# Output projections of two token blocks as seven quarter products, with bias additions ahead of the query norms

## What is computed

```python
h = rms_norm(x, g1);  q | k | v | p = h @ w_in
a = windowed_attention(rms_norm(q), rms_norm(k), v, sinks)        # 2048 x 512
m = multiscale_pool(p, pool_w, pool_b, pool_scale)                # 2048 x 512
x = x + concat([a, m]) @ w_out                                    # w_out 1024 x 1024
x = x + conv_glu(rms_norm(x, g2), w_up, conv_w, conv_b, w_down)   # d_ff 2816
```

## Time and profile before

| what | value |
|---|---|
| median of 3 runs | 1769.95 us (1769.0 to 1771.88) |
| profiled execution | 1768.54 us |
| its span, first to last instruction | 1766.7 us |
| busy: PE, DVE, ACT, POOL | 1755.5, 1283.8, 810.7, 311.3 us |
| granted PE clock | 1.000 over the whole span |
| DMA | 328.02 MB, 186 GB/s on average |

### The profile page before, as it was taken

One profiled execution on the slowest core, in us unless ns is written; L12 is line 12 of the kernel. 1 busy time (PEld: TensorE's weight loads), 2 busy tenths in 40 slices (PEclk: granted clock), 3 DMA queues, 4 the chain that ended last, 5 costly groups with the idle time before them and its releaser, 6 DMA issues.

```text
span 1766.7 us, 23461 instructions
## 1 busy us (share of the span) xinstructions
PE 1755.5 (99%) x8502; PEld 1463.1 (83%) x8502; DVE 1283.8 (73%) x1725; ACT 810.7 (46%) x1440; POOL 311.3 (18%) x296
## 2 busy tenths in 40 slices
PE   9999999999999999999999999999999999999999
PEld 7788888888888888888888888888888888888887
DVE  4645634635789888889888878878878778765774
ACT  4554544534765444444554444444444433333321
POOL 2355224216110000000000000000004023210210
PEclk9999999999999999999999999999999999999999
DMA  8865382484446433332375232232237999976884
GB/s 325 279 230 187 110 322 105 175 305 141 166 168 241 152 96 120 131 96 72 132 267 186 84 94 74 78 94 79 72 97 241 339 363 313 309 252 220 295 286 131
DMA packets 214323, 328.02 MB, mean 186 GB/s; under 512 B 13945, under 2 KB 106305, under 8 KB 214209
## 3 DMA queue, kind: packets, MB, share of 16 engines
q1 hardware_dynamic: 194782, 274.04, 46.7%
q10 hardware_dynamic: 19427, 52.49, 7.5%
HBM read 254.13 MB, written 72.35 MB: 185 GB/s over the span
## 4 chain that ended last, share of the span: by engine, by line
PE 95%; ACT 2%; DVE 1%; POOL 1%; DMA 0%; issue 0%; SPq 0%; ACTq 0%; DVEq 0%
PE ps L879 31%; PE ps L881 30%; PE ps L880 30%; ACT xs L1363 1%; PE ps L1080 1%; PE ps L1130 1%; PE ps L1067 1%; PE ps L1056 1%; PE ps L951 0%; DVE w_lo L1652 0%; DMA raw<-in_w_in_dram 0%; POOL ss_q L2171 0%; PE ps L1043 0%; POOL rstd L2171 0%; DVE mx L1843 0%
## 5 line engine op out<-in xcount | busy, mean ns | idle before, releaser
L879 PE MATMUL ps<-va_hi,wv 128*128 128x512 f32 x1232 | 479.4, 389 | 0.0
L881 PE MATMUL ps<-va_hi,wv 128*128 128x512 f32 x1232 | 479.3, 389 | 0.0
L880 PE MATMUL ps<-va_lo,wv 128*128 128x512 f32 x1232 | 479.3, 389 | 0.0
L881 PEld LDWEIGHTS ps<-va_hi,wv 128*128 128x128 f32 x1232 | 231.3, 188 | 48.1
L879 PEld LDWEIGHTS ps<-va_hi,wv 128*128 128x128 f32 x1232 | 231.3, 188 | 48.0
L880 PEld LDWEIGHTS ps<-va_lo,wv 128*128 128x128 f32 x1232 | 231.3, 188 | 47.7
L879 PE MATMUL ps<-dt_hi,ds_hi 128*128 128x512 f32 x616 | 239.6, 389 | 0.0
L880 PE MATMUL ps<-dt_lo,ds_hi 128*128 128x512 f32 x616 | 239.6, 389 | 0.0
L881 PE MATMUL ps<-dt_hi,ds_lo 128*128 128x512 f32 x616 | 239.6, 389 | 0.0
L1975 DVE SCALAR_TENSOR_TENSOR cb<-ub,cst,cb 128x1024 f32<-128x1024 f32 x176 | 218.9, 1285 | 7.8 <-ACT cb L1489 7.8
L1489 ACT ACTIVATE cb<-ub,cst 128x1024 f32<-128x1024 f32 x88 | 109.3, 1244 | 157.6 <-DVE ub L2024 91.7
(11 more groups left out here) (186 smaller groups left out, 2821.3 us busy)
## 6 DMA issues: line engine op xcount, KB each, us to landing
dg<-gT_d SPq DMA_DIRECT2D x264, 256.0 KB, 5.2
rw<-in_w_up_dram SPq DMA_DIRECT2D x84, 512.0 KB, 5.1
dw<-in_w_down_dram SPq DMA_DIRECT2D x132, 256.0 KB, 5.5
gT_d<-cb ACTq DMA_DIRECT2D x44, 512.0 KB, 2.6
w_hi<-wA_d SPq DMA_DIRECT2D x30, 512.0 KB, 4.1
w_lo<-wA_d SPq DMA_DIRECT2D x30, 512.0 KB, 5.8
raw<-in_w_out_dram SPq DMA_DIRECT2D x20, 512.0 KB, 4.5
n<-in_x_dram SPq DMA_DIRECT2D x16, 512.0 KB, 7.5
```

The lines of the kernel that those rows point to most:

```text
L879: pe.matmul(out_ap, l_hi, r_hi, start=first, stop=False, skip_group_check=True)
L880: pe.matmul(out_ap, l_hi, r_lo, start=False, stop=False, skip_group_check=True)
L881: return pe.matmul(out_ap, l_lo, r_hi, start=False, stop=last, skip_group_check=True)
```

## The change

Blocks 1 and 2 no longer take the eight units of `o`. With the block's activations as two token halves by two channel halves, and w_out as four quarters of 512 x 512, the product is formed from seven products of quarters (`product`), of 24 matmuls each (12 per pair of weight rows). Three of them use quarters of the weights as they are (`w`, products 0, 1 and 6, with a split for each of six units); four use sums of weight quarters (`tp`, products 2 to 5). Banks carry running sums from one product to the next, and DVE adds a bank to the result 14 times per block, where it was 8 (`added`).

The sums of the weights are made once, in block 1's step, one 128-row piece at a time: SP loads the piece (`to_load`), DVE forms four sums (`to_sum`), ACT and DVE their halves (`to_hi`, `to_lo`), and SP stores both to DRAM (`tO_d`, `to_store`). In the steps 2 and 3 SP brings them back into the space of the input's transpose (`tb`), which is free once the query projection is done.

The sums of the activations are made for each block on DVE: six operations of 128 x 1024 (`lefts`) and four halves (`halves`). To have the attention's result in full precision, one more copy of it per tile goes to `qT`.

POOL's additions of the bias for blocks 1 and 2 (`rb`) move from behind the query norms to the second unit of the query projection, and no longer wait for a split. Those for block 3 move behind its softmax. The loads for the convolution block (`first_loads`) are listed later.

```diff
+            units("lefts", a - 1, (0,))
...
+            units("lefts", a - 1, (1,))
+            units("halves", a - 1, (0,))
         units("q", a, (1,))
         if a == 1:
             units("r_load", a, ())
+        if a > 1:
+            units("rb", a - 1, ())
         units("win", a, (3,))
         if more:
             units("n1sc", a + 1, ())
+        if a > 1:
+            units("halves", a - 1, (1,), (2,))
         units("q", a, (2,))
         if a == 1:
+            units("to_load", a, (0,))
             units("bias", a, ())
+            units("to_sum", a, (0,))
+            units("to_hi", a, (0,))
...
-        units("rb", a - 1, ())
+        if a == 1:
+            units("rb", a - 1, ())
+            units("o", a - 1, (0, 0))
+            units("to_lo", a, (0,))
+            units("o", a - 1, (0, 1))
+            units("kt", a, ())
+            units("o", a - 1, (0, 2))
+            units("to_load", a, (1,), (2,))
+            units("to_sum", a, (1,))
+            units("qt", a, ())
+            units("to_hi", a, (1,))
+            units("to_sum", a, (2,))
+            units("to_hi", a, (2,))
+            units("o", a - 1, (0, 3))
+            units("to_store", a, (0,))
+            units("s", a, (0,), (1,))
+            units("to_lo", a, (1,), (2,))
+            units("o", a - 1, (1, 0))
+            units("inv", a, (0,))
+            units("o", a - 1, (1, 1))
+            units("s", a, (2,), (3,))
+            units("join", a, (0,), (1,))
+            units("o", a - 1, (1, 2), (1, 3))
+            units("to_store", a, (1,), (2,))
+            units("inv", a, (1,))
+        else:
+            units("w", a - 1, (0, 0), (0, 1), (1, 0))
+            units("kt", a, ())
+            units("w", a - 1, (1, 1))
+            units("tb", a - 1, (0,), (1,), (2,), (3,))
+            units("qt", a, ())
+            units("halves", a - 1, (3,))
+            units("tp", a - 1, (2, 0))
+            units("s", a, (0,))
+            units("tp", a - 1, (2, 1), (3, 0))
+            units("s", a, (1,))
+            units("inv1", a, (0,))
+            units("tp", a - 1, (3, 1), (4, 0))
+            units("s", a, (2,))
+            units("inv1", a, (1,))
+            units("tp", a - 1, (4, 1))
+            units("join", a, (0,))
+            units("tp", a - 1, (5, 0))
+            units("s", a, (3,))
+            units("tp", a - 1, (5, 1))
+            units("w", a - 1, (6, 0))
+            units("join", a, (1,))
+            units("w", a - 1, (6, 1))
+            units("tb", a - 1, (4,), (5,), (6,), (7,))
+            units("inv", a, (1,))
...
+            def tb(b, u):
+
+                slot, k = u % T_SLOTS, 2 * (u % 2)
+                if u < T_SLOTS:
+                    sp.wait_ge(S["unit_used"], used("q", b + 1, 3))
+                else:
+                    sp.wait_ge(S["out_done"], tb_used(b, u - T_SLOTS))
+                r_, c = W_SUM[2 + u // 2]
+                for half, dst in enumerate((hT_hi, hT_lo)):
+                    sp.dma_start(as_f32(dst[:, 2 * slot:2 * slot + 2, :]),
+                                 tO_d[:, half, k:k + 2, r_, c * 512:(c + 1) * 512]).then_inc(vv_in[slot], 16)
+
+            def to_load(a, j):
+
+                sp.wait_ge(S["fold_out"], 16 * 2 * KEEP)
+                if j == 0:
+                    sp.wait_ge(S["mix_done"], NT)
+                elif j < 3:
+                    sp.wait_ge(S["unit_used"], used("q", a, 3))
+                else:
+                    sp.wait_ge(S["fold_out"], T_PAST)
+                sp.dma_start(as_f32(t_low[j][:, 0, :]), w_out_v[:, j, :]).then_inc(dg_in[RING + j % 2], 16)
+                sp.dma_start(as_f32(t_low[j][:, 1, :]), wP_d[:, j, :]).then_inc(dg_in[RING + j % 2], 16)
+
+            def to_store(a, j):
+                sp.wait_ge(S["fold_lo"], LO_FROM[j] + 1)
+                for half, src in enumerate((t_high, t_low)):
+                    sp.dma_start(tO_d[:, half, j], as_f32(src[j][:])).then_inc(S["fold_out"], 16)
...
+            def product(b, i, k, hi, lo):
+                def left(kt, t):
+                    first, second = tokens(t), tokens(2 + t)
+                    return {0: (cat_hi[:, 4 + kt, first], cat_lo[:, 4 + kt, first]),
+                            1: (cat_hi[:, kt, first], cat_lo[:, kt, first]),
+                            2: (cat_hi[:, kt, second], cat_lo[:, kt, second]),
+                            3: (so[:, 0, kt, first], so[:, 1, kt, first]),
+                            4: (cat_hi[:, 4 + kt, second], cat_lo[:, 4 + kt, second]),
+                            5: (cat_hi[:, kt, first], cat_lo[:, kt, first]),
+                            6: (s4_hi[:, kt, first], s4_lo[:, kt, first])}[i]
...
+            def w(b, n, i, k):
+                split(n + LEAD)
+                if k == 1:
+                    added(b, i, 0)
+                    added(b, i, 1)
...
+            def to_sum(a, j):
+                dve.wait_ge(dg_in[RING + j % 2], 32 * (j // 2 + 1))
+                b11, b12 = as_f32(t_low[j][:, 0, 0:512]), as_f32(t_low[j][:, 0, 512:])
+                b21, b22 = as_f32(t_low[j][:, 1, 0:512]), as_f32(t_low[j][:, 1, 512:])
+                for i, (dst, x_, y_) in enumerate(((b11, b12, b11), (b12, b22, b12), (b22, b22, b11), (b21, b21, b22))):
+                    if i:
+                        dve.wait_ge(S["fold_lo"], SUM_FROM[j] + i)
+                    v.tensor_tensor(dst, x_, y_, ALU.subtract).then_inc(S["fold_lo"], 1)
+
+            def to_lo(a, j):
+                dve.wait_ge(S["fold_hi"], BIAS_FOLDED + j + 1)
+                v.tensor_tensor(t_low[j][:], as_f32(t_low[j][:]), as_f32(t_high[j][:]), ALU.subtract
+                                ).then_inc(S["fold_lo"], 1)
...
+                if part == 0:
+                    dve.wait_ge(S["aT_lo"], NT * b + NT)
+                    dve.wait_ge(S["aT_hi"], NT * b + NT)
+                    dve.wait_ge(S["mT_ready"], 4 * b + 4)
+                    dve.wait_ge(S["mix_done"], NT * b + NT)
+                    step(0, sx[:, 0], a2, m(cat_hi, SECOND), ALU.add)
+                    step(1, sx[:, 0], sx[:, 0], m(cat_lo, SECOND), ALU.add)
+                    step(2, a2, a1, a2, ALU.subtract)
+                else:
+                    step(3, a1, sx[:, 0], a1, ALU.subtract)
+                    step(4, sx[:, 1], m(cat_hi, FIRST), a1, ALU.subtract)
+                    step(5, sx[:, 1], sx[:, 1], m(cat_lo, FIRST), ALU.add)
...
             def rb(a):
                 if a == 0:
                     pool.wait_ge(S["fold_copied"], BIAS_COPIED)
-                if a < NB - 1:
                     split_there(pool, SPLIT_NO[UNIT["o", a, 0, 2]])
                 pool.wait_ge(r_in[a % 2], 16 * (a // 2 + 1 + (a % 2 == 0)))
                 for t in range(NT):
```

230 lines of the change are left out of this document (185 added, 45 removed).

## The result

The changed kernel takes **1841.1 us** (1838.6 to 1843.57, 4 runs), against 1770.89 us for the kernel before on the same chip: a ratio of 1.0397, with a 95% interval of 1.0385 to 1.0410. The sign was forecast, the size was not: +70 us instead of +32, outside the range of 1777 to 1817.

A forecast was written before the change was run, and what follows sets the result against it. PE's work plus its waits was taken as the bound. Step 1 +7, block 1 +14.3, block 2 +11.2 and block 3's additions +1.5 made +34.0 on 1768.54, about 1804 against the median, rounded down to 1802 us; range 1777 to 1817.

The forecast's parts named there:

- What is taken away: Output projections of blocks 1 and 2: 48 matmuls fewer save 10.9 us, 5.45 per block.
- What is put on DVE: Sums and subtractions ahead of block 1's first weight split add 11.0 us on DVE; PE would wait 2.7 us, undisturbed.
- the bias additions disturb: POOL's four additions hold DVE 9.1 us ahead of the first split; PE waits 11.8 us in block 1.
- Rival (a): DVE is never held by POOL; first waits 2.7 and 0 us, total 1785.8 us; chance 0.20.
- The third unit: Its split, behind the query norms on DVE, comes too late: 6.2 us more waiting in each of blocks 1 and 2.
- The DRAM traffic of the sums themselves: Weight sums, 8 MB out and 16 MB back, run while DMA engines are half idle; costed at nothing.
- Rival (d): Loads of the sums come late in both blocks, 2 x 6.5 us, total 1815 us; chance 0.03.
- the keys: Key copies on ACT, behind the fifth unit's split, are some 1.4 us late for the query transposes, per block.
- Block 3's own additions: On POOL they stand ahead of block 2's second norm; some +1.5 us at block 2's first transposes (0 to 3).
- The clock: PE's clock slowing after five waits of over 4 us could cost 0 to 13.5 us; taken as 0.
- Rival (c): PE's clock falls after each long wait, five times up to 2.7 us more, about 1814 us; chance 0.08.
- step 1: Forming the weight sums in block 1's step delays the third split and the evictions: +7 us, 2 to 8.

The follow-up runs named there:

- e14: Best kernel: e11's order without POOL's added wait, block 3's bias additions in two halves, block 2's moved beside step 3's second key unit; 1765.6 us, ratio 0.9970.
- e4: e3 with POOL's bias additions of blocks 1 and 2 put back behind the query norms; 1806.43 us, ratio 1.0200.
- e5: e3 with the six operand sums and first two low halves on DVE moved ahead of the key norm, bias additions left in place; 1801.05 us, ratio 1.0164.
- e1: Changed kernel with the store of the fourth weight sums moved on SP behind the kept weights' loads; 1832.83 us, ratio 1.0355.
- c1: e3 with unused matmuls filling PE's waits in blocks 1 and 2 (44 and 32 ahead of the first product, 24 at two later places); 1823.84 us, ratio 1.0301.
- e6: e5 with the third and fourth splits among DVE's query norms, product 6's splits later, and key transposes ahead of the third unit; 1785.28 us, ratio 1.0070.
- e2: Changed kernel with the convolution block's first loads moved behind the raw loads of block 3's third and fourth output units; 1837.44 us, ratio 1.0381.
- e3: Changed kernel with both the store of the fourth weight sums and the convolution block's first loads moved later; 1824.54 us, ratio 1.0303.
- e9_and_step1: e6 with bias additions re-placed, block 3's x loaded later, and in step 1 the first high half later and third split among the norms; 1773.97 us, ratio 1.0016.
- e11: e10 with step 1's weight sums and halves spread over its units and the first sums' store behind the next raw load; 1773.69 us, ratio 1.0014.
- e10: e9_and_step1 with POOL's additions for block 3 made to wait until DVE has scaled block 2's second norm; 1778.25 us, ratio 1.0039.

## Why the prediction was right in sign and wrong in size

**What is taken away: right.** 48 records fewer. With nothing late, a projection should take 50.24 - 5.45 = 44.8 us; step 2 of e14 takes 45.8.

**What is put on DVE, and the bias additions disturb: right.** 11.8 us forecast, 10.39 measured in step 2; 9.1 and 7.55 in step 3. e4 and e5 show both halves of the cause. An addition takes 2.34 us by the spacing of block 3's, which run alone, where the working had 2.27. The Trainium skill (SBUF — State Buffer, Who interferes with whom), by which one engine holds the shared ports for its whole instruction, agrees with the rows here: four sums in 11.3 us. Rival (a) falls.

**The third unit: right.** From the end of the first wait to the end of the second the forecast had 5.45 + 6.2 = 11.65 us; measured are 323.63 - 312.01 = 11.62. Only 4.05 of it show as a wait, because the 24 matmuls between took 2 us more at the lower clock.

**First failed step: "The DRAM traffic of the sums themselves ... I cost it at nothing."** It weighed bytes and the cover of the loads back. The cost was in the order of SP's queue: a store that waits for DVE, ahead of loads that wait for nothing. 15.8 us, over a fifth of the whole. e1 shows that the store was it: 13.1 of them go with it. Rival (d), late loads of the sums, did not occur. The Trainium skill (DMA: Bandwidth & Descriptors, Anatomy of one DMA — SWDGE (gpsimd) path) has the half of this that mattered: a semaphore wait is served by the sequencer that issues, before dispatch. The trace agrees for SP's queue: 25.3 us of waiting for DVE ahead of the store's issue. The prediction had this order for the store of the first sums, in step 1, and didn't follow the fourth, which comes after that step.

The traffic cost something in a second place, at the keys. They were given 1.4 us. From the third unit's start to the query transposes 11.5 us pass (335.13 - 323.63), where the work between takes 6.1 (c1, at full clock): 5.4 late, part of it hidden under the slow matmuls. The raw weights of the fifth unit, asked for behind 4 MB of sums, were used 8.7 us after their issue, where the working had 3.9 from the kernel before. e6 takes this high half away from the keys, and their wait goes; that the loads ahead of it made it late is read from the trace alone.

**Second: the moved loads were given no term.** They cost 9.15 us of waiting and what the clock lost behind it. That stretch became 10.2 us longer, where the sum had 1.5 for "Block 3's own additions". Even the 1.5 was too small: 3.80 us once the larger wait is gone (e2). In the profile of e2 the last stretch is only 4.6 us shorter, which is this covering; that its whole is less still goes with its longer step 1.

**Third: "The clock ... I take 0, since no row in mid-run shows a slower pace."** No row could, as the kernel before had no long wait. Rival (c) was right in its mechanism: the granted clock is 0.50 behind the waits of 12.2 and 10.4 us. 24 matmuls lose 2 to 2.8 us there. The Trainium skill (TensorE: Matmul & The Clock Gate, Part 1), that an idle PE falls back to 1.2 GHz, agrees. But its cost isn't a sum over waits: c1 puts it at some 3 us for e3's steps 2 and 3, since a late split or key absorbs the slow matmuls ahead of it.

**Fourth, mis-sized: step 1,** +10.2 instead of 7. The third split was over at 170.3, not 167.6, and PE waited 3.98 us for it instead of 2.1, with 2.6 us of slow pace behind; the wait at the evictions was 3.08 instead of 4.3. ACT's first high half (1.92 us) stands ahead of the second unit's, for which DVE then waited 2.93 us; the working had only DVE's own sums there.

```profile
155.72 1.92 ACT L1570 ACTIVATE t_high<-t_low 128x2048 fp32r<-128x2048 f32 x1 [3.17 <-DVE t_low L2022]
157.55 1.04 ACT L1410 ACTIVATE w_hi<-raw 128x1024 fp32r<-128x1024 f32 x1
```

By stretch (forecast, measured): step 1 +7, +10.2; ahead of step 2's query projection 0, +15.8; step 2's projection with its first wait +14.3, +19.4; step 3's +11.2, +16.3; after it +1.5, +10.2. The 5 us more in step 2 are, by the trace, the later keys (+4.0), the slow transposes and 12 matmuls behind them (+1.6) and about 1 that e14 has as well (45.8 against 44.8), less 1.4 at the first wait; step 3 looks alike. Of the forecast's own numbers one doesn't follow from its terms: rival (a) with step 1 at its lower bound is 1785.8 - 5 = 1780.8, not 1777. No result hangs on it.

**Open.** The prediction's had DVE unhindered beside an addition of 2.84 us, and here additions hold sums that wait for each other and splits that don't (e4). What sets that pair apart wasn't tried. In e9_and_step1 and e11 several moves of step 1 were made at once, so what each gave there isn't known. How much of step 1 varies from one execution to the next for the same order (60.4 and 63.8 us) has only those profiles behind it.

## What to carry to other kernels

When an order is changed, walk the queue that issues DMAs like an engine: an issue that waits for a computation costs every load behind it its lead, whatever the bytes. Removing a wait shows the next one under it, so two edits at different queues are measured together before either is called small. And a product that saves PE's work pays only once the sums that it needs find room in time that other engines spend idle: here the same matmuls gave 1841 us in one order and 1766 in another.

## What the runs showed of the hardware

- An addition of 128x1024 on POOL (2.34 us alone) holds splits on DVE that are independent of each other as well as chained sums: two splits took 6.05 us instead of 2.36 (e4), one sum of 0.7 us took 2.90, four scalings 7.82 instead of 2.74 (e9_and_step1, e10).
- After a wait of 10 to 12 us TensorE's granted clock was 0.50, and 24 matmuls took 7.4 to 8.2 us instead of 5.4; behind one of 3.98 us they took 8.1. With matmuls in the waits it read 1.00 (c1).
- Raw weights, issued behind other loads (3 MB), were used 15 us after their issue, where loads of that size landed in 5.5 us by the median of the page; behind 4 MB they were used 8.7 us after it.
